# One more empty step at two places of each delta-rule head in two interleaved streams

## The reference

```python
def gated_delta_rule(q, k, v, beta, log_decay):
    cum = jnp.cumsum(log_decay, axis=-1)
    decay_mat = masked_exp(cum[..., :, None] - cum[..., None, :], incl)
    kk = jnp.einsum('bhnid,bhnjd->bhnij', k, k)
    a_strict = jnp.where(strict, beta[..., :, None] * kk * decay_mat, 0.0)
    t_mat = a_strict + jnp.eye(c, dtype=q.dtype)
    rhs = jnp.concatenate([v * beta[..., None], k * (beta * jnp.exp(cum))[..., None]], -1)
    sol = lax.linalg.triangular_solve(t_mat, rhs, left_side=True, lower=True, unit_diagonal=True)
    u, w = sol[..., :v.shape[-1]], sol[..., v.shape[-1]:]
    attn = jnp.einsum('bhnid,bhnjd->bhnij', q, k) * decay_mat
    ...
    def step(s, xs):
        v_new = u_c - w_c @ s
        o = qi_c @ s + attn_c @ v_new
        s = s * last_c + ks_c.T @ v_new
...
def diag_decay_linear_attention(q, k, v, log_a):   # S_t = diag(a_t) S_{t-1} + k_t v_t^T
    cum = jnp.cumsum(log_a, axis=-2)
    rel = masked_exp(cum[i] - cum[j], incl)
    attn = jnp.einsum('bhid,bhjd,bhijd->bhij', q_c, k_c, rel)
...
def gated_rms_heads(o, gate, g, n_heads):
    oh = oh * lax.rsqrt(jnp.mean(jnp.square(oh), -1, keepdims=True) + RMS_EPS) * g
    return oh * jax.nn.silu(gate)
...
    log_f = jnp.logaddexp(log_lb, jnp.log1p(-lb) + jax.nn.log_sigmoid(cf))     # HGRN's decay
```

## Time and profile before

| | |
|---|---|
| median of 3 runs | 3547.36 us (3541.97 to 3564.09) |
| the profiled execution | 3551.67 us, its span 3549.9 us |
| PE busy | 3151.6 us (89% of the span) |
| DVE, ACT, POOL busy | 1649.2, 1222.9 and 834.3 us |
| mean granted clock of PE | 0.911 of full speed |
| mixer stage | from 1704 to 2437 us of the span |

### The profile page before, as it was taken

One profiled execution on the slowest core, in us unless ns is written; L12 is line 12 of the kernel. 1 busy time (PEld: TensorE's weight loads), 2 busy tenths in 40 slices (PEclk: granted clock), 3 DMA queues, 4 the chain that ended last, 5 costly groups with the idle time before them and its releaser, 6 DMA issues.

```text
span 3549.9 us, 63807 instructions
## 1 busy us (share of the span) xinstructions
PE 3151.6 (89%) x26726; PEld 2658.3 (75%) x26726; DVE 1649.2 (46%) x2883; ACT 1222.9 (34%) x2083; POOL 834.3 (24%) x808
## 2 busy tenths in 40 slices
PE   7778898889898999999798888888989999789887
PEld 6767787778678999999576666666769998545565
DVE  4544544455524344341444464556566556432332
ACT  2423332333322233232424343533254343332341
POOL 4121122112112100000445454552000002513232
PEclk9988897889869999999999898999999999778898
DMA  3111111111004233332112121223325555301111
GB/s 124 28 31 31 31 38 32 28 29 44 26 28 160 78 115 91 92 91 66 51 54 63 48 69 54 60 60 139 95 71 172 166 162 178 119 17 45 42 45 60
DMA packets 93935, 260.45 MB, mean 73 GB/s; under 512 B 10672, under 2 KB 10672, under 8 KB 92240
## 3 DMA queue, kind: packets, MB, share of 16 engines
q1 hardware_dynamic: 81072, 209.17, 20.0%
q0 software_dynamic: 7680, 35.66, 2.9%
q10 hardware_dynamic: 4896, 11.54, 0.9%
HBM read 236.27 MB, written 20.05 MB: 72 GB/s over the span
## 4 chain that ended last, share of the span: by engine, by line
PE 73%; DVE 12%; ACT 9%; issue 3%; DMA 2%; POOL 1%; DVEq 0%; ACTq 0%; SPq 0%; POOLq 0%
PE psum L429 71%; DVE arena L361 6%; ACT arena L346 5%; DVE arena L370 3%; ACT arena L354 3%; PE psum L433 2%; DMA ring<-in_w 1%; ACT L342 1%; DVE arena L365 1%; ACT L346 1%; DVE arena L382 1%; POOL arena L361 1%; DVE arena L392 0%; DMA arena<-in_x 0%; DVE arena L373 0%
## 5 line engine op out<-in xcount | busy, mean ns | idle before, releaser
L429 PE MATMUL psum<-arena,ring 128*128 128x264 f32 (+3 forms) x7720 | 1652.3, 337 | 18.4 <-DVE arena L361 10.4
L429 PEld LDWEIGHTS psum<-arena,ring 128*128 128x128 f32 (+1 forms) x7720 | 1257.7, 194 | 173.7 <-issue 36.0
L429 PE MATMUL psum<-arena 32*32 32x32 f32 (+14 forms) x12708 | 972.0, 258 | 286.7 <-ACT arena L346 71.7
L429 PEld LDWEIGHTS psum<-arena 32*32 32x32 f32 (+9 forms) x12708 | 685.3, 144 | 541.1 <-issue 220.2
L429 PE MATMUL psum<-arena,arena 128*128 128x264 f32 (+2 forms) x5440 | 1008.4, 301 | 33.7 <-DVE arena L361 12.7
L429 PEld LDWEIGHTS psum<-arena,arena 128*128 128x128 f32 x5440 | 802.0, 189 | 86.9 <-issue 32.2
L354 ACT ACTIVATE arena<-psum 128x512 f32<-128x512 f32 (+14 forms) x660 | 302.1, 458 | 767.1 <-PE psum L429 627.7
L373 POOL CAST ring<-ring 128x512 fp32r<-128x512 f32 x332 | 222.9, 671 | 1241.8 <-DMA ring<-in_w 1233.0
L361 DVE TENSOR_TENSOR arena<-arena 128x528 f32<-128x528 f32 (+9 forms) x638 | 366.2, 574 | 228.7 <-ACT arena L346 123.1
L361 DVE TENSOR_TENSOR ring<-ring,arena 128x1024 fp32r<-128x1024 f32 (+1 forms) x250 | 293.5, 1174 | 349.5 <-ACT arena L354 346.9
L361 POOL TENSOR_TENSOR ring<-ring,ring 128x512 fp32r<-128x512 f32 x332 | 444.2, 1338 | 26.7
(11 more groups left out here) (48 smaller groups left out, 962.1 us busy)
## 6 DMA issues: line engine op xcount, KB each, us to landing
ring<-in_w SPq DMA_DIRECT2D x202, 512.0 KB, 3.5
ring<-in_w SPq DMA_DIRECT2D x356, 256.0 KB, 2.7
bg<-arena ACTq DMA_DIRECT2D x24, 256.0 KB, 2.0
yd<-arena ACTq DMA_DIRECT2D x10, 512.0 KB, 4.5
arena<-in_x SPq DMA_DIRECT2D x2, 2112.0 KB, 11.5
arena<-bg POOLq DMA_DIRECT2D x1, 3072.0 KB, 16.5
od<-arena POOLq DMA_DIRECT2D x8, 264.0 KB, 2.4
oy<-arena POOLq DMA_DIRECT2D x8, 264.0 KB, 2.3
```

The lines of the kernel that those rows point to most:

```text
L429: self.last_ins = self.eng.matmul(out, l, r, start=start, stop=stop, skip_group_check=skip)
```

## The change

Five functions' worth of streams get one `yield` more at two places of each head: between the decay row and the turning of A, and between the last output product and the sum of its squares. The same two places are changed on PE, ACT and DVE, so that the rounds still correspond. No instruction of arithmetic is added or removed, and no wait.

```diff
@@ pe_mixers, delta
             P.did("gd_row", hd)
             yield
+            yield
             P.wait_ge(*at("gd_A", hd))
@@
             P.drop(bo)
+            yield
             yield
             P.colsum(("gd_osum", hd), ("gd_oroot", hd), c["ones"], [U.n1], T, [("gd_osq", hd)])
```

## The result

Measured over 20 executions each, the changed kernel takes 3565.74 us in the median (3556.33 to 3574.75), the kernel before 3549.1 (3540.23 to 3564.09). The ratio is 1.0044, with a 95% interval of 1.0035 to 1.0054: some 16 us slower, where 12 us faster was forecast. The profiled execution, 3556.33 us, was the fastest of the twenty.

The account below looks back on a forecast made before the run. PE bounds the kernel, busy 89% of the span, with about 122 us of waits in the changed stage. Terms -3.6 +1.3 -0.3 +0 +2 -17.2 +5 gave -12.8 off the median 3547.36: 3535 us (chance 0.50), range 3506 to 3563.

Parts of the forecast that it names:

- Head 0: Head 0's turning of A: wait falls from 4.24 to 1.9, nine following matmuls speed up; -3.6 us (-4.2 to -2).
- Head 1: Decay row moves into run 1's first level; two waits, 10.0 together, become one of 11.6; +1.3 us (-3 to +7).
- Softplus chains: PE's waits ahead of run 2 and behind the chains of runs 2 to 5 shrink; -17.2 us (bounds 0 and -29).
- Head 2: Head 2's turning of A and Y: 8.6 against 8.0 and some 0.8 of slow clock; -0.3 us (-4 to +3).
- Head 3: Decay chain moves between two of run 4's levels; 13.4 after against 13.5 before; 0 us (-4 to +7).
- the end: Rounds 148 to 152: four rounds won, -2; six splits ahead of awaited state products, +7; +5 us (0 to +9).
- A wait costs more than itself: PE's clock falls to 1.2 GHz behind a wait; at head 0 the nine matmuls behind lost 1.84 us on top.
- head 1's inversion slides into run 1's tail: Part of the shift elsewhere: -2 us there, in a term of +2 us (-6 to +9).
- the waits move and do not shrink: Rival: chains on DVE and ACT keep their length and stop PE at the next place; 3547 us, chance 0.19.
- The slower rival: Decay chains of heads 1 and 3 delay levels in full; 3556 to 3569, middle 3562 us; chance 0.18.
- the 4.6 in the upper bound: POOL blocking DVE's four decay-chain operations at heads 1 and 3: 4.6 us in the upper bound, 0 in the sum.

Follow-up runs that it names:

- e9: Kernel before the change, with `delta` seven steps ahead of `linear` in place of six, every head one round earlier; 3532.81 us, ratio 0.9943 to the kernel before.
- e12: Changed kernel, with head 2's four projections in eight steps in place of twelve, on PE, ACT and DVE; ratio 1.0019 to the kernel before.
- e7: Changed kernel plus 21 unused 128x512 matmuls on PE, three ahead of each of seven products of head 1's inversion; ratio 1.0043 to the kernel before.
- e11: Changed kernel, with `delta` nine steps ahead of `linear` in place of six; ratio 1.0034 to the kernel before.
- e2: Kernel before plus only the empty step between last output product and squares' sum, in all four heads; ratio 1.0098 to the kernel before.

## Why the prediction was wrong

**Head 0.** The wait fell to 2.20 as worked out (1.9). The clock didn't come back: the next six matmuls take 2.91 us, where six at the rate of the 18 ahead of the wait take 1.5. Rounds 6 to 20 gained 2.2, not 3.6, and a new wait of 2.35 at the end of head 0 took most of it.

**Head 1.** Right: one wait of 10.07 at the first level, forecast 11.6, in place of the two of before. (The term's own figures, 11.6 less 10.0, give +1.6 and not +1.3.)

**Softplus chains, the largest term.** The waits went down by less than counted: 5.65 became 2.97, 7.96 became 4.88, 7.00 became 4.61, 6.15 became 5.75, 8.03 became 7.47, together 34.8 down to 25.7 where the forecast's figures add up to 21.2. And the term contained "with the clock", and the clock gave nothing: rounds 66 to 75 lost 5.8 in place of 5.1. And the prediction said of the second place that there was nothing to win, on the rows of heads 0 and 2. The waits of 7.96 and 8.03 stand at this very matmul in heads 1 and 3, behind ACT's copy and square, which stand behind the chain. I had read them as the chains' own. In the changed kernel head 1's sum stands in round 76 and doesn't wait, but the recurrence ahead of it now waits behind the chain (4.88). In e9, with the whole of `delta` one round earlier, the copy and the square stand ahead of the chain and neither waits.

**Head 2: the place that failed most.** "8.6 against 8.0", -0.3. Measured: waits +3.6, clock loss +2.1 in rounds 84 to 90, and 1.7 more of it just ahead. The 5.4 fits what it says of `linear`'s squares behind ACT's decay chain, and came out right: 5.68. What the 1.7 stood for the prediction doesn't say; a wait at `gd_kk` is not named in it, and it is 6.95, since PE has little besides head 2's projections in rounds 84 to 87 and comes to `gd_kk` long before DVE has scaled k. In e12, where `gd_kk` is back in round 84, that wait is gone and the rounds' waits are 5.1 shorter.

**Head 3, the end.** 0 and +5 forecast; +1.6 of waits in rounds 119 to 131, and +1.0 of waits and +1.9 of clock in 149 to 162, where the second traces have +1.9 and +1.1. The price of a decay chain in a level (one wait of 6.84) was right.

**The clock: the step that turned the sign.** The prediction let the clock into the sum only as a surcharge on waits ("A wait costs more than itself"), so it had to come out below zero with the waits. Measured it is +11.6, with waits of +1.7. 4.5 of it arise in rounds 59 to 65 where PE hardly waits; e7 and the table by shift tie it to the narrow work that stands there. I had put those rounds down as "head 1's inversion slides into run 1's tail, which has waits of its own (-2)": the waits there did fall, by 0.4, at a price of 4.5 in clock loss.

Of the rivals, "the waits move and do not shrink" describes the waits exactly (118 to 120), but priced that at no change. The slower rival named the decay chains in the level loop. It had two chains paid in full, 14.2 us of waits, where the stage's waits grew by 1.7 to 3.0 in all. That its 3562 came near is luck. My range ended at 3563, 3 us short.

The Trainium skill, "TensorE: Matmul & The Clock Gate", section "HAM oscillation — how this bites in real kernels", tells of gaps that bring the clock down. The low stretches of rounds 84 to 90 agree (they begin within the waits of 6.95 and 5.68). That of rounds 59 to 65 begins behind a wait of 2.52 but lasts for 20.5 us of which PE is busy for 20.13, and e7's begins behind none: for these gaps are no explanation, and the traces decide. That DVE was held by POOL in the moved chains, by the Trainium skill, "SBUF — State Buffer", section "Who interferes with whom", would have shown in their products on DVE. These take 0.69 us each at heads 1 and 3 after the change, as they did before, for POOL stands idle there (18.70 us at head 1, 6.94 at head 3) beside nearly all of them. So the 4.6 in the upper bound had nothing to stand on in this order.

## What stays open

How much of the 16 us each place has: e12 gives 9 (3 to 15) to the place of heads 2 and 3, the clock in run 1's tail is 4.5 by the traces, and the rest is below what a ratio tells. No run brings that 4.5 back as time: e7 spends it on the added work, and e11 on waits elsewhere. Why e2 costs 35: in its trace the stage is 30 us longer than before, 9 of them waits and 21 PE's busy time, but why its clock is so often low isn't shown. Nor is it shown what brings the clock down at 1992.30, the waits ahead or the narrow work. And whether it is the 32x32 products, the 64-row ones or their kind of data that let the clock fall: e7 adds wide work, it doesn't separate them.

## What to carry to other kernels

When two streams share PE, look at what stands side by side, not only at what waits: a stretch of narrow matmuls with nothing wide in between can run at half clock while PE is 99% busy, and the total of PE's busy time for the same matmuls, between two traces, shows it at once. Before moving a consumer later, look at which long waits stand at it in every repetition, not in two of four: here two of the longest stood at the place that was moved later, and the whole stream one step earlier, without any other change, made the kernel 20 us faster (ratio 0.9943). In a fixed interleaving, the lead of one stream over the other is a single number worth trying in both directions before any single step is touched.

## What the runs showed of the hardware that I had not expected

The clock loss of a stage came out alike in two executions of one order, 44.5 and 45.5, then 56.1 and 57.2, and in rounds 59 to 65 within 0.1. A PE that was busy for 20.13 of 20.50 us with narrow matmuls, but for one sum of squares, stayed at 1.2 GHz throughout. With 15 wide ones among 171 records the piece had a granted 0.77 in place of 0.55, and there the clock fell after 11 us without a wait over 0.12.
